# The convolved tiles and retention's v are stored to scratch by ScalarE instead of SyncE

## The reference

```python
def mixer_block(hn, ...):
    proj = hn @ w_in
    gq, gk, gv, gz, ga, gb, rq, rk, rv, rg, gate_a, gate_b = jnp.split(proj, SPLIT_IDX, axis=-1)
    qkv = silu(causal_dwconv(concat([gq, gk, gv]), conv_w))    # 4 taps along the tokens
    o_a = gated_delta_chunked(l2norm(gq), l2norm(gk), gv, log_g, beta)
    rq, rk = rotary(rq, pos), rotary(rk, pos)
    o_b = retention_chunked(rq, rk, rv)
    y = sigmoid(gate_a) * rms(o_a) * silu(gz) + sigmoid(gate_b) * silu(rg) * rms(o_b)
    return y @ w_out

h = h + mixer_block(rmsnorm(h, norm1), ...)
h = h + conv_ffn(rmsnorm(h, norm2), ...)       # up to 2 x 2816, conv of 3, silu(a) * b, down
h = rmsnorm(h, norm_f)
```

## Time and profile before

| | |
|---|---|
| median of 3 runs | 2186.41 us (2184.21 to 2188.30) |
| the profiled execution | 2188.12 us, of which the span of the trace is 2186.3 us |
| TensorE busy | 2105.0 us, 96% |
| VectorE, ScalarE, GpSimd busy | 1126.8, 642.8, 296.9 us |
| mean granted TensorE clock | 0.984 of full speed |
| DMA | 209 MB, mean 96 GB/s |

### The profile page before, as it was taken

One profiled execution on the slowest core, in us unless ns is written; L12 is line 12 of the kernel. 1 busy time (PEld: TensorE's weight loads), 2 busy tenths in 40 slices (PEclk: granted clock), 3 DMA queues, 4 the chain that ended last, 5 costly groups with the idle time before them and its releaser, 6 DMA issues.

```text
span 2186.3 us, 30706 instructions
## 1 busy us (share of the span) xinstructions
PE 2105.0 (96%) x13268; PEld 2024.6 (93%) x13268; DVE 1126.8 (52%) x1276; ACT 642.8 (29%) x811; POOL 296.9 (14%) x283
## 2 busy tenths in 40 slices
PE   7999999889999999899999999999999999999995
PEld 6999999889999999889999999999999999999984
DVE  3443554556555655445443434265656556565564
ACT  4222324433334443333443333321111111111113
POOL 0000002578700212112100001100000000000004
PEclk9999999989999999999999999999999999999997
DMA  7232225554343544335324231121111101111002
GB/s 203 82 105 88 84 93 184 183 161 136 110 146 112 174 133 138 92 102 155 107 78 185 82 109 52 39 83 34 49 49 58 49 30 49 57 51 49 30 30 77
DMA packets 137882, 209.00 MB, mean 96 GB/s; under 512 B 12748, under 2 KB 98196, under 8 KB 137620
## 3 DMA queue, kind: packets, MB, share of 16 engines
q1 hardware_dynamic: 137748, 207.04, 29.7%
HBM read 153.49 MB, written 53.52 MB: 95 GB/s over the span
## 4 chain that ended last, share of the span: by engine, by line
PE 85%; DVE 5%; DMA 3%; POOL 3%; issue 2%; ACT 2%; SPq 0%; DVEq 0%; POOLq 0%; ACTq 0%
PE a_psum L732 34%; PE a_psum L139 28%; PE a_psum L1016 11%; PE a_psum L800 1%; POOL ext L1792 1%; POOL y L1788 1%; DMA y<-mix_scratch 1%; DMA ext<-mix_scratch 1%; PE a_psum L717 1%; PE a_psum L844 1%; PE a_psum L818 1%; PE a_psum L740 1%; PE a_psum L925 1%; PE a_psum L828 1%; PE a_psum L797 1%
## 5 line engine op out<-in xcount | busy, mean ns | idle before, releaser
L732 PE MATMUL a_psum<-xh,w_hi 128*128 128x348 f32 (+1 forms) x1896 | 617.8, 326 | 4.8 <-ACT post L1130 3.7
L732 PE MATMUL a_psum<-xl,w_hi 128*128 128x348 f32 (+1 forms) x1896 | 611.0, 322 | 0.0
L732 PE MATMUL a_psum<-xh,w_lo 128*128 128x348 f32 (+1 forms) x1896 | 608.6, 321 | 0.0
L732 PEld LDWEIGHTS a_psum<-xh,w_hi 128*128 128x128 f32 x1896 | 359.0, 189 | 7.9 <-ACT post L1130 4.6
L732 PEld LDWEIGHTS a_psum<-xl,w_hi 128*128 128x128 f32 x1896 | 359.0, 189 | 0.7
L732 PEld LDWEIGHTS a_psum<-xh,w_lo 128*128 128x128 f32 x1896 | 358.7, 189 | 0.0
L1130 ACT ACTIVATE post<-a_psum 128x348 f32<-128x348 f32 (+1 forms) x234 | 107.2, 459 | 646.3 <-PE a_psum L732 615.3
L1062 ACT ACTIVATE w_hi<-w_raw 128x1024 fp32r<-128x1024 f32 x131 | 138.3, 1056 | 433.1 <-PE a_psum L139 409.4
L139 PE MATMUL a_psum<-xh,w_hi 128*128 128x342 f32 (+1 forms) x1104 | 234.8, 321 | 6.2 <-DVE xl L1359 6.2
L139 PE MATMUL a_psum<-xl,w_hi 128*128 128x342 f32 (+1 forms) x1104 | 234.9, 321 | 0.0
L139 PE MATMUL a_psum<-xh,w_lo 128*128 128x342 f32 (+1 forms) x1104 | 234.2, 320 | 0.0
(11 more groups left out here) (210 smaller groups left out, 2602.5 us busy)
## 6 DMA issues: line engine op xcount, KB each, us to landing
w_raw<-in_w_in SPq DMA_DIRECT2D x79, 512.0 KB, 3.7
mix_scratch<-post SPq DMA_DIRECT2D x48, 522.0 KB, 2.8
w_raw<-in_w_up SPq DMA_DIRECT2D x44, 512.0 KB, 3.5
ext<-mix_scratch SPq DMA_DIRECT2D x9, 1536.0 KB, 8.5
y<-mix_scratch SPq DMA_DIRECT2D x27, 512.0 KB, 6.4
down_raw<-in_w_ffn_down SPq DMA_DIRECT2D x22, 512.0 KB, 4.4
ext<-grow_scratch SPq DMA_DIRECT2D x9, 512.0 KB, 5.8
ext<-mix_scratch SPq DMA_DIRECT2D x9, 512.0 KB, 7.2
```

The lines of the kernel that those rows point to most:

```text
L732: mm = pe.matmul(psum[:, u % 2, 0:n], w[:, k, :], x[:, k, at0 + n * j:at0 + n * j + n], start=(k == 0 and part == 0), stop=(k == KC - 1 an ...
```

## The change

The 24 stores of convolved tiles and the 8 of retention's v are issued by ScalarE: the first directly behind SiLU, after a wait for SiLU's own end, the second at the step "rvstore", after a wait for the copy out of PSUM. They count on two new semaphores, `kept`. The 16 stores of rotated tiles stay with SyncE and count on `stored`. Whoever waited for both kinds waits for both semaphores. No other instruction is added or taken out, and no buffer changes.

```diff
-        stored = [sem(f"stored{s}") for s in range(2)]
+        stored, kept = ([sem(f"{n}{s}") for s in range(2)] for n in ("stored", "kept"))
...
             def stored_up_to(t):
                 for n in range(2):
-                    sp.wait_ge(stored[n], 16 * (8 + sum(1 for m in range(T_K, t + 1) if m % 2 == n)))
+                    sp.wait_ge(stored[n], 16 * 8)
+                    sp.wait_ge(kept[n], 16 * sum(1 for m in range(T_K, t + 1) if m % 2 == n))
...
-                elif kind == "rvstore":
-                    t = a[0]
-                    store(t, S_RV + t - T_RV, evac, 3 * t + 3)
...
-                elif kind == "silu":
-                    t = a[0]
-                    slot = S_K + t - T_K if t < T_RV else S_Q + t - T_Q if t < T_V else S_V + t - T_V
-                    store(t, slot, a_silu, convs_before(t) + 1)
...
+            def free_stage(t):
+                act.wait_ge(stored[t % 2], 16 * 8)
+                if t - T_K >= 2:
+                    act.wait_ge(kept[t % 2], 16 * ((t - T_K) // 2))
...
                     act.wait_ge(d_conv, 4 * q + 4)
-                    act.wait_ge(stored[t % 2], 16 * stores_before(t))
+                    free_stage(t)
                     act.activation(st[t % 2][:, FRONT:T], acc[:, 0:T - FRONT], ACT.Silu).then_inc(a_silu, 1)
+                    act.wait_ge(a_silu, q + 1)
+                    act.dma_start(sc["mix"][S_K + t - T_K if t < T_RV else S_Q + t - T_Q if t < T_V else S_V + t - T_V, :,
+                                            LEAD:TW], st[t % 2][:, :]).then_inc(kept[t % 2], 16)
+                elif kind == "rvstore":
+                    t = a[0]
+                    act.wait_ge(evac, 3 * t + 3)
+                    act.dma_start(sc["mix"][S_RV + t - T_RV, :, LEAD:TW], st[t % 2][:, :]).then_inc(kept[t % 2], 16)
...
-                        pool.wait_ge(stored[1], 16 * 24)
+                        pool.wait_ge(kept[1], 16 * 16)
```

More of the change, by code:

```diff
@@ L318, in front_plan @@
     return plan
-def stores_before(t):
-    return t // 2 if t < T_AB else 8 + (t - T_K) // 2
 def convs_before(t):
```

## The result

The changed kernel takes 2190.69 us (median of 20 runs, 2187.02 to 2192.64), the kernel before 2186.67 us on the same chip (median of 20 runs, 2183.39 to 2189.20). The ratio is 1.0017, 95% interval 1.0010 to 1.0024: slower by about 4 us. The interval tells this from no change, though it is little: the medians of before differ by 1.7 us from job to job. The forecast was 2189.9 us, +3.5.

A forecast was written before the change was run, and what follows sets the result against it. TensorE, busy 96% of the span, was taken to bound the kernel; 0.35 + 0.45 + 2.5 + 1.7 - 1.5 = +3.5 us on the median 2186.41 gave 2189.9 us, range 2183.5 to 2197.5 us.

The forecast's parts named there:

- SyncE's freedom: SyncE's queue: losing 32 issues (10.6 us) and 71.6 us of waits for SiLU gains next to nothing, taken as 0.
- rival 3: Faster: DMAs share at no cost, the 0.84 us idle at 700 us goes, low clock shrinks; -4.9 us, 2181.5 us, chance 0.10.
- The issue of tile 28's store: On ScalarE between chunk 2's copies and the split of weights at 380.58 us: the issue costs +0.35 us.
- The store behind SiLU of tile 46: On ScalarE ahead of the table load at 742.13 us: issue and wait for SiLU's end cost +0.45 us.
- rival 2: ScalarE held in its issue: the store at 742 us takes 3.16 us, not 0.4; +6.2 us, 2192.6 us, chance 0.08.
- Sharing: Stores of tiles 27, 29 and 32 slow critical v-tile loads by 1.0, 1.0 and 0.5 us, together +2.5 us.
- rival 1: Full sharing: three stores each delay their load 2.1 us, clock falls twice more; +9.0 us, 2195.4 us, chance 0.30.
- The clock: TensorE in the v tiles: first idle time grows to 2.6 us, bringing one more fall of the clock, +1.7 us.
- The tap: VectorE's convolution of tile 48 at 765 us: GpSimd's L1821 finishes before the taps, gaining -1.5 us.
- Rival 4: V stores go later, not earlier, behind steps ScalarE waits for (tile 27 at 363.5 us); already in the sum, no chance given.

The follow-up runs named there:

- silu_only: Changed kernel with only the 24 stores of convolved tiles, behind SiLU, issued by ScalarE, the others by SyncE; 2189.31 us, ratio 1.0004 to the kernel before.
- v_only: Changed kernel with only the 8 stores of retention's v issued by ScalarE, the 24 of convolved tiles by SyncE; 2188.12 us, ratio 1.0001 to the kernel before.
- t27: Changed kernel with only the store of tile 27 issued by ScalarE, all others by SyncE; 2188.55 us, ratio 1.0006 to the kernel before.
- v_three: Changed kernel with only the stores of v tiles 27, 29 and 32 issued by ScalarE; 2190.36 us, ratio 1.0014 to the kernel before.
- t27_twice: Only tile 27's store issued by ScalarE, plus a second store of the same row to an unread scratch; 2189.91 us, ratio 1.0018 to the kernel before.
- early_sp: Kernel before, all stores with SyncE, with SyncE's m_load loads issued one unit earlier, ahead of the previous chunk's `mst`; 2171.21 us, ratio 0.9922.

## Why the prediction was right

The time, its size and its sign came out: 2190.69 for a forecast of 2189.9 us. The terms did not all, and I go through them in the order of the sum.

- **SyncE's freedom, 0.** Right: 71.6 us of waits are gone, and none of it shows. The idle time of 0.84 us at 700 us is gone in after as well, as rival 3 had it, but also in silu_only, v_only and t27; the last moves no store near it, so its absence is no effect of the change.
- **The issue of tile 28's store, +0.35 us.** Wrong, it is 0. The store is issued at 380.33 us beside the copies, which end at 383.03 us, and the split starts at 383.05 us. I took the place in the order for a place in time. The same error made me put tile 27's store at 363.5 us; it went at 361.71 us, in front of the load.
- **The store behind SiLU of tile 46, +0.45 us.** Right: the table load waits for 0.39 us and no longer 0.02. ScalarE was never held in its issue, 0.35 us at most: rival 2 is out.
- **Sharing, +2.5 us.** Right in sum, 2.65 us in the pieces; wrong in its parts. Tile 27: forecast 1.0, measured 1.55 us. Tile 29: forecast 1.0, measured about 0. Its store was issued at 393.99 us, but its packets came only behind m_load 4 (7.3 us from 391.60 us; 7.2 in before, 7.0 in t27). The weights of 392.43 us took 7.97 us and m_load 4's place on the chain; but the idle time there is the same 3 us with and without this store (after 3.02, t27 2.93). Tile 32: forecast 0.5, measured 1.1 us (6.88 for 5.77). Half of a store was the wrong share, of the wrong size: a store takes 1.3 us of the DMA engines, not 2.1, and the load grew by 1.6 us for one and by 2.6 us for two, the whole of each. The Trainium skill ("DMA: Bandwidth & Descriptors", "Queues, rings and completion order") has the engines take turns between the queues by packets. For tile 27's store the trace agrees; tile 29's took no turn in the 4.7 us from its issue to 398.7 us, and there it does not. So rival 1 had the share right for tile 27's store and nearly for tile 32's, and its price, 2.1 us a store, wrong.
- **The clock, +1.7 us.** The fall I forecast came in each trace with tile 27's store on ScalarE, 3.4 us at 371 us. What I missed is that the delay has a return: the next idle time shrank by 1.6 us and the low stretch behind it held less work, so steps 2 and 3 together came to -0.85 us. Stretches of low clock there are as many as before, 3.3 to 3.4 us three times (the 6.8 us of before counts as two).
- **The tap, -1.5 us.** Wrong: -0.07 us. I had left out that the first instruction of the convolution can be slowed by GpSimd as well as the second, and that the store would land late from the new queue too.

My sum of +3.5 us is therefore partly luck: by what was measured it is 0 + 0.37 + 2.65 (1.55 and 1.1) - 0.85 - 0.07 = +2.1 us on this one pair of executions, and the two terms that missed by most, the clock and the tap, missed in opposite directions. The traces of after and before stand 2.03 us apart at the end of that convolution (773.14 in after, 771.11 in before). But 0.9 us of this are from before the first moved store, so only 1.1 us are the pair's own; the 0.84 us of idle time at 700 us, which after lacks, is most of what is missing from the 2.1. The interval of the runs is +2.2 to +5.2 us, so the pair lies below it, and about half of the 4 us of the medians is in no piece that I can name.

A part of it goes with the clock. The granted clock, as a mean over the runs, is 0.9841 or 0.9842 in after, v_three and t27_twice, the three of these nine kernels whose interval shows a loss, and 0.9846 to 0.9854 in the six others; 0.001 is 2.2 us here. In the v tiles of the profiled pair there is no more low clock than before, so it lies elsewhere, and no run shows where or why. v_only, with all three harmful stores, has 0.9854 and measures +0.7 us, v_three +2.9 us.

Rival 1's sum, 2195.4 us, lies outside the interval. Rival 3 is refuted by the runs. Rival 4 stands on its head: the stores of tiles 27 and 32 didn't go later than before, as I had said, but earlier, measured from the issue of `mst` (0.01 and 0.02 us behind it in after, 1.67 and 1.68 us in before).

What stays open is the loss on top of early_sp, 4 to 5 us with no m_load on the chain, and the half of the change's own loss that goes with the clock. The longer loads and idle times are shown; that they are the whole loss is not. One rival of "the second queue" is untested too: tile 27's and tile 32's stores went ahead of their loads, where before they stood behind them. No run puts a store ahead of the load in SyncE's own queue, which could cost the same.

## What to carry to other kernels

Before a store moves to a second queue, list the loads of the first queue that the chain waits for and look at what moves at the same time: behind such a load in its own queue a store cost it half a microsecond at most here (7.04 us with one at 415.71 us in before, 6.54 us without at 417.81 us in after); issued ahead of it from another queue it cost the load about the whole 1.3 us that it takes of the DMA engines, and issued 2.4 us behind it, 0.3 us at most. A wait of 71.6 us on a queue says nothing by itself; what was worth 17 us was the place of another step in the same queue, which the chain of waits named at once. And a delay on one turn of a loop can be repaid at the next, so that a cost per place must not be multiplied by the places.

## What the hardware did that I had not expected

- ScalarE's queue issues a DMA while activations ahead of it in the order still run: 361.71 us beside copies from 361.70 to 364.4 us. Such an issue cost the engine nothing; one that must wait for the activation itself cost 0.37 us (an idle time of 0.39 for one of 0.02 us).
- During the load of m_load 2 the DMA engines were 0.92 busy in before already (361.6 to 368.8 us), so there was no room for a free ride. This load of 512 KB went from 7.1 to 8.7 to 9.7 us with none, one and two stores of 522 KB beside it, while the v stores' own median went down from 7.5 to 4.7 us: what the stores gained, the loads paid.
- A store in a queue of its own can still wait: tile 29's was issued at 393.99 us and moved nothing until 398.7 us, while the other queue had loads under way.
- VectorE's instruction with one tensor input, L1404, took 2.21 us beside GpSimd's L1822, and the same instruction in before 0.76 us without. It lost 1.45 us, the tap with two inputs 1.52 us (2.83 for 1.31).
- The stretches of low clock beyond 745 us don't fall at the same places in all executions, between 745 and 749 us in before (granted clock 0.57 there, 1.00 in after) and between 774 and 778 us in after (0.57, and 1.00 in before). With up to 1.7 us for each, they can make a good part of the 3 us of scatter, and a difference of 1 us between two traces is worth nothing until it is found at its place.
